# Two-layer transformer blocks on one core: the norms' roots taken on two columns of tokens, and the first blocks of a stage multiplied chunk by chunk

## The chip, the cores and the metric

The kernel runs on one core of one Trainium2 chip. The metric is the device time of one execution in microseconds. The engines named here are TensorE (PE in the profile; its weight loads are the rows PEld), VectorE (DVE), ScalarE (ACT), GpSimd (POOL) and the DMA queue of SyncE (SP).

## The reference, cut to what matters

Two small networks follow one another on 256 tokens of width 1024. Each has two layers, and each layer is: half an ffn, a mixer, half an ffn. Every one of these six parts of a network starts from an RMS norm of the residual stream; the first network also scales and shifts by a modulation vector, and the second ends with one more norm.

```python
def rmsnorm(x, g):
    y = x * lax.rsqrt(jnp.mean(x * x, axis=-1, keepdims=True) + EPS)
    return y * g

def adaln_in(x, g, m, i):
    return rmsnorm(x, g) * (1 + m[:, i, 1][:, None]) + m[:, i, 0][:, None]

def swiglu(h, w1, w3, w2):
    return (jax.nn.silu(h @ w1) * (h @ w3)) @ w2
...
for l in range(DEPTH):
    x = x + 0.5 * m[:, 0, 2] * swiglu(adaln_in(x, norm_g[l, 0], m, 0), ...)
    h = adaln_in(x, norm_g[l, 1], m, 1) @ w_in[l]
    mix = mixer_ab(h, ...) if l % 2 == 0 else mixer_cd(h, ...)
    x = x + m[:, 1, 2] * (mix @ w_out[l])
    x = x + 0.5 * m[:, 2, 2] * swiglu(adaln_in(x, norm_g[l, 2], m, 2), ...)
```

## The kernel before

The work is a list of twelve stages, `STAGES`: ffn, ab, ffn, ffn, cd, ffn for the first network (0 to 5), and ffn, hy, ffn, ffn, sw, ffn for the second (6 to 11). `NSTAGE` (12) is the final norm. The residual `x` lies in SBUF with the 1024 features as 8 chunks of 128 partitions and the 256 tokens in the free direction. The engines run programs of their own, written out by hand and joined by semaphores; there is no scheduler.

**Weights** come as a stream of triples (three blocks of 128 x 1024 f32). SyncE issues a triple into one of two landing places when the one before has been split; ScalarE rounds each block to bf16 (`split_high`, `ring_hi`), VectorE takes the difference (`split_low`, `ring_lo`), and TensorE forms each product as three bf16 products (`product`, lines 392 to 394). The activations are split in the same way into `h_hi` and `h_lo`, `a_hi` and `a_lo`. In stages 0, 2, 3 and 5 VectorE also works off blocks of the modulation weights (`mod_block`).

**A norm of stages 1 to 5 and 12.** As the residual's chunks are updated, ScalarE squares them (`squares`), and TensorE sums the squares over the features with a product of all-ones weights, `sumsq`: eight products of 256 columns into the PSUM bank `pssq`, whose every row then holds the sums of the 256 tokens. VectorE scales them and adds epsilon (line 1192), takes the reciprocal (1193), ScalarE takes the square root (`root`, line 924), and VectorE multiplies `x` by the gain and by `rs` chunk by chunk (line 1330). ScalarE rounds each chunk to `h_hi` (with the shift as its bias), VectorE writes `h_lo` (1335), and TensorE waits for each chunk's `h_ready`. When the stage before is an ffn, two blocks of a ring triple are split ahead of the squares and one behind them. The norm of stage 0 is done by itself at the start. The norms of stages 6 to 11 (`deferred`) multiply by the root only after the product; nothing changes in them.

**An ffn** has 22 steps j. `up(j)` multiplies two weight blocks with h, 24 products of 256 columns for each block, into one of three banks; two steps behind, `down(j)` adds to the eight accumulators. In a deferred ffn step 0 is `up_first`, which takes for each chunk of h the products of both blocks; in stages 0, 2, 3 and 5 step 0 is `up(0)`: the eight chunks for the first block, then the eight for the second.

**Around the two mixers.** Ahead of stage 1 (ab) TensorE makes four products of the bias tables (`filter_start`, line 408), which ScalarE copies out (`bias_rows`, 909); ScalarE also copies out the projected chunks (1071), and a chunk from the third on waits for such a copy. Ahead of stage 4 (cd) TensorE makes a product for the norm of a long filter (431) and its spectrum, eight products of 512 columns (439), before it projects the first chunk; VectorE and ScalarE need both later in the stage.

## Time and profile before

| | |
|---|---|
| median of 3 runs | 2114.94 us (2112.21 to 2116.51) |
| the profiled execution's time | 2119.04 us |
| its span | 2117.3 us |
| TensorE busy | 1912.7 us, 90% |
| VectorE busy | 1436.4 us, 68% |
| ScalarE busy | 989.7 us, 47% |
| DMA | 423.98 MB, mean 200 GB/s |
| mean granted TensorE clock | 0.949 |

### The profile page before, as it was taken

The numbers are of one execution on the slowest core, as the hardware profiler recorded it, in microseconds if no ns is written. First come the engines' busy times: TensorE is split into PE (matmuls) and PEld (weight loads), VectorE is DVE, ScalarE is ACT, GpSimd is POOL, SyncE is SP. The second block draws the span as 40 slices with busy tenths as digits, with TensorE's granted clock in tenths as the row PEclk, the third lists the DMA queues.
The fourth block names the chain that finished last, engine by engine and source line by source line (L and its number), as shares of the span: only waits on it lengthen the run. The fifth ranks groups of instructions, "written<-read, shape, count | busy, mean of one in ns | idle before, by whom it ended". The sixth has DMA issues, their size and how long they took to land.

```text
span 2117.3 us, 38192 instructions
## 1 busy us (share of the span) xinstructions
PE 1912.7 (90%) x16458; PEld 1634.7 (77%) x16458; DVE 1436.4 (68%) x2248; ACT 989.7 (47%) x1591; POOL 6.5 (0%) x14
## 2 busy tenths in 40 slices
PE   3999878999999984799999998779999999969998
PEld 2888667888788862478888887547888888858887
DVE  6889675878798845566576666554766766765664
ACT  3444644445544540344455454324544545464543
POOL 0000000000000000000000000000000000000000
PEclk7999989999999996899999999779999999989999
DMA  8989432776699540336656554203555555432552
GB/s 322 390 339 362 175 149 98 291 281 239 241 366 360 224 182 0 120 143 226 234 181 223 195 193 179 91 30 120 196 195 207 182 207 209 152 118 91 217 200 80
DMA packets 54276, 423.98 MB, mean 200 GB/s; under 512 B 5955, under 2 KB 6131, under 8 KB 26683
## 3 DMA queue, kind: packets, MB, share of 16 engines
q1 hardware_dynamic: 52172, 413.59, 51.9%
q0 software_dynamic: 1936, 7.95, 1.0%
q8 instruction: 130, 2.13, 0.4%
q14 instruction: 38, 0.31, 0.0%
HBM read 420.38 MB, written 1.13 MB: 199 GB/s over the span
## 4 chain that ended last, share of the span: by engine, by line
PE 70%; DVE 16%; ACT 6%; DMA 5%; issue 2%; SPq 0%; DVEq 0%; ACTq 0%
PE pw L392 14%; PE pw L393 14%; PE pw L394 14%; PE acc L392 7%; PE acc L394 7%; PE acc L393 7%; DVE ring_lo L1349 6%; DMA land<-stream 4%; ACT ring_hi L1001 2%; DMA modw<-wmod 1%; PE acc L617 1%; DVE modw L1244 1%; PE pw L582 1%; PE pssq L460 1%; PE pw L585 1%
## 5 line engine op out<-in xcount | busy, mean ns | idle before, releaser
L392 PE MATMUL pw<-h_hi,ring_hi 128*128 128x256 bf16 x3248 | 892.8, 275 | 55.0 <-DVE h_lo L1335 36.5
L393 PE MATMUL pw<-h_lo,ring_hi 128*128 128x256 bf16 x3248 | 892.7, 275 | 0.0
L394 PE MATMUL pw<-h_hi,ring_lo 128*128 128x256 bf16 x3248 | 892.5, 275 | 0.0
L1349 DVE TENSOR_TENSOR ring_lo<-land,ring_hi 128x1024 bf16<-128x1024 f32 x633 | 737.6, 1220 | 191.9 <-ACT ring_hi L1001 191.4
L1001 ACT ACTIVATE ring_hi<-land 128x1024 bf16<-128x1024 f32 x633 | 622.1, 1045 | 234.6 <-DMA land<-stream 120.8
L392 PEld LDWEIGHTS pw<-h_hi,ring_hi 128*128 128x128 bf16 x3248 | 318.5, 98 | 118.8 <-issue 53.1
L392 PE MATMUL acc<-a_hi,ring_hi 128*128 128x256 bf16 x1408 | 384.9, 273 | 4.4 <-DVE a_lo L1399 4.4
L394 PE MATMUL acc<-a_hi,ring_lo 128*128 128x256 bf16 x1408 | 384.8, 273 | 0.0
L393 PE MATMUL acc<-a_lo,ring_hi 128*128 128x256 bf16 x1408 | 384.8, 273 | 0.0
L394 PEld LDWEIGHTS pw<-h_hi,ring_lo 128*128 128x128 bf16 x3248 | 319.7, 98 | 39.8
L393 PEld LDWEIGHTS pw<-h_lo,ring_hi 128*128 128x128 bf16 x3248 | 318.9, 98 | 38.5 <-issue 0.3
L1244 DVE SCALAR_TENSOR_TENSOR modw<-modw,condb 128x1024 f32<-128x1024 f32 x144 | 171.4, 1220 | 13.3 <-DMA modw<-wmod 12.9
L392 PEld LDWEIGHTS acc<-a_hi,ring_hi 128*128 128x128 bf16 x1408 | 137.8, 98 | 21.7 <-DVE a_lo L1399 5.3
L393 PEld LDWEIGHTS acc<-a_lo,ring_hi 128*128 128x128 bf16 x1408 | 137.8, 98 | 16.4
L394 PEld LDWEIGHTS acc<-a_hi,ring_lo 128*128 128x128 bf16 x1408 | 137.8, 98 | 16.5
L1006 ACT ACTIVATE gu<-gu 128x256 f32<-128x256 f32 x88 | 36.7, 417 | 236.3 <-DVE gu L1390 236.3
L1011 ACT ACTIVATE a_hi<-gu 128x256 bf16<-128x256 f32 x176 | 73.3, 416 | 135.1 <-DVE gu L1397 135.1
L1399 DVE TENSOR_TENSOR a_lo<-gu,a_hi 128x256 bf16<-128x256 f32 x176 | 75.0, 426 | 84.8 <-ACT a_hi L1011 84.8
L1009 ACT ACTIVATE gu<-pw 128x256 f32<-128x256 f32 x88 | 33.2, 377 | 127.0 <-PE pw L394 127.0
L1390 DVE TENSOR_TENSOR gu<-pw,rs 128x512 f32<-128x512 f32 x88 | 60.7, 690 | 42.3 <-PE pw L394 42.3
L1397 DVE TENSOR_TENSOR gu<-gu,pw 128x256 f32<-128x256 f32 x88 | 36.7, 417 | 49.8 <-ACT gu L1009 49.5
L1157 ACT ACTIVATE prob<-pw,nbias 128x256 f32<-128x256 f32 (+1 forms) x48 | 20.6, 433 | 105.5 <-DVE nbias L1526 105.5
(230 smaller groups left out, 1557.7 us busy)
## 6 DMA issues: line engine op xcount, KB each, us to landing
land<-stream SPq DMA_DIRECT2D x211, 1536.0 KB, 6.5
modw<-wmod SPq DMA_DIRECT2D x144, 512.0 KB, 7.6
biasT<-bias_rows POOLq DMA_DIRECT2D x3, 1536.0 KB, 9.1
biasT<-bias_rows POOLq DMA_DIRECT2D x1, 3072.0 KB, 13.2
cst_s<-cst SPq DMA_DIRECT2D x1, 1792.0 KB, 10.1
x<-xT SPq DMA_DIRECT2D x1, 1024.0 KB, 9.7
out<-proj SPq DMA_DIRECT2D x1, 1024.0 KB, 3.9
par_s<-par SPq DMA_DIRECT2D x1, 699.0 KB, 13.8
```

The costliest lines, as they stand in the source:

```text
L392: mm(o, lhs[0], rhs[0], start=start, stop=False, skip_group_check=True)
L393: mm(o, lhs[0], rhs[1], start=False, stop=False, skip_group_check=True)
L394: return mm(o, lhs[1], rhs[0], start=False, stop=stop, skip_group_check=True)
L1001: fn(ring_hi[:, t % RING, b, :], land[:, t % LAND, b, :], ACT.Copy).then_inc(hi_ready, 1)
L1006: fn(sig[:, j % 2, :], sig[:, j % 2, :], ACT.Silu).then_inc(silu_done, 1)
L1009: fn(sig[:, j % 2, :], pw[j % (LAG + 1)][:, 0:S], ACT.Silu).then_inc(silu_done, 1)
L1011: fn(a_hi[:, j % (LAG + 1), :], act_in[:, j % 2, :], ACT.Copy).then_inc(a_hi_ready, 1)
L1244: v.scalar_tensor_tensor(modw[:, k % MODR, :], modw[:, k % MODR, :], 1.0, condb[:], ALU.mult, ALU.mult, accum_out=macc[:, g % 2, k:k + 1]) ...
L1349: v.tensor_tensor(ring_lo[:, t % RING, b, :], land[:, t % LAND, b, :], ring_hi[:, t % RING, b, :], ALU.subtract).then_inc(lo_ready, 1)
L1390: v.tensor_tensor(gu[:, j % 2], pw[j % (LAG + 1)][:].rearrange("p (b s) -> p b s", b=2), rs[:].unsqueeze(1).to_broadcast([P, 2, S]), ALU.m ...
L1397: v.tensor_tensor(act_in[:, j % 2, :], sig[:, j % 2, :], up_half, ALU.mult).then_inc(gated_ready, 1)
L1399: v.tensor_tensor(a_lo[:, j % (LAG + 1), :], act_in[:, j % 2, :], a_hi[:, j % (LAG + 1), :], ALU.subtract).then_inc(act_ready, 1)
```

## The change

For the norms of stages 1 to 5 and the final one (`columns(n)`), the squares become the stationary operand and a single column of ones the moving one: the sums come out as two columns, a token to a partition. ScalarE takes the root of scale times sum plus epsilon from PSUM in one instruction, VectorE takes the reciprocal of the 128x2 result, multiplies the identity by each column (`dg`), and TensorE multiplies all-ones weights with these two diagonals (`spread_root`), which puts the inverse root back as rows into `pssq`. The multiplies with the gain read `pssq` instead of `rs`. `spread_root` stands right behind `sumsq` for the ffn stages and the final norm; in stage 1 behind the first of the four table products, in stage 4 between the filter's norm product and its spectrum.

Step 0 of the ffn stages 0, 2, 3 and 5 becomes `up_first`, with a wait for the last ffn's gated halves. In stage 1 the first two projected chunks are made by `first_chunks`, for each chunk of h the products of both.

```diff
             def sumsq(n):
                 for k in range(KD):
                     pe.wait_ge(sq_ready, KD * n + k + 1)
-                    m = mm(pssq[:, 0:S], ones[:], sq[:, k, :], start=(k == 0), stop=(k == KD - 1))
+                    if columns(n):
+                        for tt in range(TT):
+                            m = mm(pssq[:, tt:tt + 1], sq[:, k, tt * P:(tt + 1) * P], ones[:, 0:1],
+                                   start=(k == tt == 0), stop=(k == KD - 1), skip_group_check=True)
+                    else:
+                        m = mm(pssq[:, 0:S], ones[:], sq[:, k, :], start=(k == 0), stop=(k == KD - 1))
                 m.then_inc(ssq_ready, 1)
+            def spread_root(n):
+                pe.wait_ge(diag_ready, column_no(n))
+                for tt in range(TT):
+                    m = mm(pssq[:, tt * P:(tt + 1) * P], ones[:], dg[:, tt, :], start=(tt == 0), stop=True, skip_group_check=True)
+                m.then_inc(bcast_mm, 1)
...
                 mm(pw[2][:], ones[:], f_sq[:, 0, :], start=True, stop=True).then_inc(filt_mm, 1)
+                spread_root(4)
                 spectrum(f_sum, f_dif).then_inc(filt_mm, 1)
...
-                    if j == 0 and deferred(i):
-                        pe.wait_ge(act_ready, f0)
+                    if j == 0:
+                        if f0:
+                            pe.wait_ge(act_ready, f0)
                         up_first()
...
+            def first_chunks(i, kind):
+                t = FIRST[i]
+                for k in range(KD):
+                    pe.wait_ge(h_ready, KD * i + k + 1)
+                    for n in range(2):
+                        if k == 0:
+                            await_triple(t, n + 1)
+                        m = product(bank_of(kind, n)[:, 0:S], weights(t, n, k, slice(0, P)), hidden(k), start=(k == 0), stop=(k == KD - 1))
+                        if k == KD - 1:
+                            m.then_inc(proj_mm, 1)
...
+            def column_root(n):
+                act.wait_ge(ssq_ready, n + 1)
+                fn(rsc[:], pssq[:, 0:TT], ACT.Sqrt, scale=1.0 / D, bias=eps_col[:, 0:1]).then_inc(root_ready, 1)
...
             def root_of(n):
-                dve.wait_ge(ssq_ready, n + 1)
-                rsqrt(("norm", n), rs[:], pssq[:, 0:S], 1.0 / D)
+                dve.wait_ge(root_ready, ROOT["norm", n])
+                done(v.reciprocal(rsc[:], rsc[:]))
+                for tt in range(TT):
+                    ins = v.tensor_scalar(dg[:, tt, :], cs("ident"), rsc[:, tt:tt + 1], None, ALU.mult)
+                ins.then_inc(diag_ready, 1)
+                dve.wait_ge(bcast_mm, column_no(n))
...
-                        v.scalar_tensor_tensor(h[:, k, :], x[:, k, :], g, rs[:], ALU.mult, ALU.mult).then_inc(affine_ready, 1)
+                        v.scalar_tensor_tensor(h[:, k, :], x[:, k, :], g, pssq[:, 0:S] if columns(n) else rs[:],
+                                               ALU.mult, ALU.mult).then_inc(affine_ready, 1)
```

## Rows read from the trace of the kernel before

**Rows 1.** The page's part 1: busy time, share of the span, instructions.
```profile
PE 1912.7 (90%) x16458; PEld 1634.7 (77%) x16458; DVE 1436.4 (68%) x2248; ACT 989.7 (47%) x1591; POOL 6.5 (0%) x14
```

**Rows 2.** Windows, stage 3: stretch, length, busy us of each engine, clock, DMA.
```profile
553.00:720.00 167.00, 167.00 (x1532) 149.45 (x1531) 147.41 (x215) 83.69 (x115) 0.00 (x0) 1.00 0.91 352
```

**Rows 3.** The chain that ended last, in the final norm: start, us, what.
```profile
2107.04 0.43 DVE rs L1192
...
2107.50 1.76 DVE rs L1193
...
2109.29 0.42 ACT rs L924
...
2109.74 0.48 DVE proj L1330
```

**Rows 4.** Timeline of stage 2's start, VectorE and TensorE: start, us, what.
```profile
353.23 0.48 DVE L1335 SCALAR_TENSOR_TENSOR h_lo<-proj,modT,h_hi 128x256 bf16<-128x256 f32 x1
...
357.18 1.27 DVE L1335 SCALAR_TENSOR_TENSOR h_lo<-proj,modT,h_hi 128x256 bf16<-128x256 f32 x3
...
353.85 0.37 PE L392 MATMUL pw<-h_hi,ring_hi 128*128 128x256 bf16 x1 [4.62 <-DVE h_lo L1335]
```

**Rows 5.** Windows over the first 48 products of stages 2, 3, 5; the end of stage 0.
```profile
353.85:362.07 8.22, 8.22 (x48) 4.97 (x49) 4.60 (x12) 4.03 (x8) 0.00 (x0) 0.66 0.62 262
544.68:553.05 8.37, 8.37 (x48) 5.03 (x49) 6.88 (x14) 4.03 (x8) 0.00 (x0) 0.65 0.09 16
917.81:925.65 7.84, 7.84 (x48) 4.76 (x49) 4.60 (x12) 4.02 (x8) 0.00 (x0) 0.69 0.01 2
219.60:222.80 3.20, 3.20 (x17) 2.27 (x16) 1.36 (x4) 2.74 (x6) 0.00 (x0) 0.50 0.93 399
```

**Rows 6.** Timeline, single series of f32 pieces on TensorE, and one of VectorE.
```profile
345.61 3.62 PE L460 MATMUL pssq<-sq,ones 128*128 128x256 f32 x16
...
1842.75 0.60 PE L452 MATMUL pssq<-ones,rs 1*128 1x1 f32 x4
...
320.39 2.05 PE L703 MATMUL acc<-gu,KR 128*128 128x128 f32 x16
...
286.73 3.78 PE L703 MATMUL acc<-gu,prob 128*128 128x128 f32 x16 [4.74 <-DVE gu L1583]
...
299.60 0.87 DVE L1583 TENSOR_SCALAR gu<-cst_s,dn 128x128 f32<-128x128 f32 x4
```

**Rows 7.** Groups of instructions by form: busy us and mean ns of one.
```profile
L1028 ACT ACTIVATE es<-nb,par_s 128x2 f32<-128x2 f32 x24 | 5.6, 279 | 0.0
...
L1537 DVE RECIPROCAL den<-den 128x2 f32<-128x2 f32 x24 | 3.9, 161 | 14.2 <-ACT prob L1157 14.2
...
L1376 DVE SCALAR_TENSOR_TENSOR x<-acc,ada,x 128x256 f32<-128x256 f32 x48 | 20.8, 479 | 24.4 <-PE acc L394 24.4
...
L1330 DVE SCALAR_TENSOR_TENSOR proj<-x,ada,rs 128x256 f32<-128x256 f32 x48 | 22.0, 478 | 2.4 <-ACT rs L924 2.4
```

**Rows 8.** Timeline of stage 1's start, TensorE and ScalarE.
```profile
228.66 3.60 PE L408 MATMUL acc<-biasT,par_s 33*8 33x512 f32 x8
...
241.89 0.62 ACT L1071 ACTIVATE proj<-pw 128x256 f32<-128x256 f32 x2
...
242.39 0.27 PE L392 MATMUL pw<-h_hi,ring_hi 128*128 128x256 bf16 x1 [1.33 <-ACT proj L1071]
```

**Rows 9.** Timeline of stage 4's start, TensorE.
```profile
724.28 1.02 PE L431 MATMUL pw<-proj,ones 128*128 128x512 f32 x2
725.14 3.60 PE L439 MATMUL acc<-qb,cst_s 128*128 128x512 f32 x8
...
732.01 0.27 PE L392 MATMUL pw<-h_hi,ring_hi 128*128 128x256 bf16 x1
```

**Rows 10.** The chain that ended last, in stage 4.
```profile
745.45 0.28 ACT proj L1124
...
745.87 0.22 PE pw L392
```

More of the change, by code:

```diff
@@ L165, in build @@
         den = sb("den", [P, 2, TT])
+        rsc = sb("rsc", [P, TT])
         esink = sb("esink", [P, 2, TT])
@@ L198, in build @@
         f_dif = prob[:].rearrange("p b t s -> p (b t s)").rearrange("p (t c) -> p t c", t=TT)
+        dg = gu[:, 0, 0:1].rearrange("p a (t q) -> p (a t) q", t=TT)
         sig, act_in = gu[:, :, 0, :], gu[:, :, 1, :]
@@ L266, in build @@
         dve_step = sem("dve_step")
+        diag_ready, bcast_mm = sem("diag_ready"), sem("bcast_mm")
         pair_s, pair_b, pair_e, pair_n = sem("pair_s"), sem("pair_b"), sem("pair_e"), sem("pair_n")
@@ L304, in deferred, with columns, column_no @@
             return 6 <= n < NSTAGE
+        def columns(n):
+            return 1 <= n < 6 or n == NSTAGE
+        def column_no(n):
+            return n if n < 6 else 6
         def seen(kind, tt):
@@ L409, in filter_start @@
                        start=True, stop=True).then_inc(filt_mm, 1)
+                    if i == 0:
+                        spread_root(1)
             def filter_layer(l):
@@ L776, in mixer_ab @@
             def mixer_ab(i):
-                for n in range(7):
+                first_chunks(i, "ab")
+                for n in range(2, 7):
                     chunk(i, "ab", n)
@@ L867, in _ @@
                     sumsq(i)
+                    if kind == "ffn":
+                        spread_root(i)
                 if kind == "ffn":
@@ L893, in _ @@
             sumsq(NSTAGE)
+            spread_root(NSTAGE)
         @block.scalar
@@ L921, in root @@
             def root(what, t):
-                act.wait_ge(recip_ready, 6 if what == "filter" else what[1] + 1 + (what[1] > 4))
+                act.wait_ge(recip_ready, 2 if what == "filter" else 1 if what[1] == 0 else what[1] - 3)
                 fn(t, t, ACT.Sqrt).then_inc(root_ready, 1)
+            def column_root(n):
+                act.wait_ge(ssq_ready, n + 1)
+                fn(rsc[:], pssq[:, 0:TT], ACT.Sqrt, scale=1.0 / D, bias=eps_col[:, 0:1]).then_inc(root_ready, 1)
             def inverse_root(dst, src, scale, step):
@@ L981, in norm @@
                         split_high(AFTER[n - 1] - 1 + AHEAD, blocks=(2,))
-                    root(("norm", n), rs[:])
+                    column_root(n)
                 for k in range(KD if n < NSTAGE else 0):
```

## Prediction

> **What bounds the kernel now.** I read the page first: TensorE is busy for 1912.7 of 2117.3 us [rows 1], so time can come only out of its pauses, or out of stretches at its lower clock. Five of the six changed norms stand where it pauses. The windows over the long stretch of the second block's ffn pair show what surrounds a norm: from 553 to 720 us TensorE is busy for 167.00 of 167.00 us at the full clock, although the DMA share is 0.91 [rows 2]. A block that starts sooner therefore ends sooner, as long as weights arrive. I then followed the chain that ended last through one norm, the final one, where nothing overlaps [rows 3]: the squares' products, VectorE's scale-and-add (0.43 us), its reciprocal over 256 elements (1.76), ScalarE's root (0.42), and the first multiply at 2109.74. From 2107.04 to 2109.74 are 2.70 us with TensorE idle. Stages 1 to 5 have the same four steps. Last I read the instructions behind a norm [rows 4]: in stage 2 the first low half is written from 353.23 to 353.71 and the last three by 358.45 (357.18 + 1.27), so the eighth chunk of h is there 4.74 us after the first, and TensorE starts at 353.85. Its first 48 products (both blocks of j = 0) take 8.22, 8.37 and 7.84 us in stages 2, 3 and 5, at a mean clock of 0.66, 0.65 and 0.69 [rows 5], where 48 at the full rate (1532 in 167.00 us is 0.109 each [rows 2]) would need 5.23.
>
> **The change, the chain of one norm.** Out go 2.70 us. In come, one behind another:
> - The sums. Before, 16 pieces (each f32 product is two) took 3.62 us [rows 6]. Now 32 pieces load a 128x128 f32 tile of squares each and move one column. Four pieces with one moving column took 0.60 us, and 16 pieces that load 128x128 and move 128 took 2.05, which gives at most (2.05 - 0.60) / 12 = 0.121 a piece [rows 6]. I take 0.115: 0.60 + 28 x 0.115 = 3.82, that is 0.20 longer. The squares are there in time, as before.
> - The root of two columns on ScalarE: 0.28, like the other 128x2 activation with a bias [rows 7]. In the late stages it is queued behind the third split of a ring block, which is done before the sums are.
> - The reciprocal of 128x2: 0.16 [rows 7].
> - Two 128x128 multiplies of the identity: four such took 0.87 [rows 6], two take about 0.48.
> - The diagonal product, four pieces: between 0.60 (one column each) and 0.60 + 0.10 for the wider ones: 0.70.
> - Handovers: each step starts 0.02 to 0.05 after the one before [rows 3]; five of them, 0.20.
>
> That is 0.20 + 0.28 + 0.16 + 0.48 + 0.70 + 0.20 = 2.02, so a norm's chain is **0.7 us** shorter. Upper bound: a piece at 0.111 and handovers of 0.02 give 0.9. Lower bound: with TensorE at its lower clock 16 pieces took 3.78 instead of 2.05 [rows 6]; four then take 0.5 more, and the gain is 0.2.
>
> The multiplies that use the root now read PSUM. The multiply-add with a PSUM source took 479 ns, the one from SBUF 478 [rows 7], so I cost this at nothing. The Trainium skill (VectorE: DVE Perf Modes, the section on the TRN2 errata) gives PSUM sources 62 cycles more of fixed time; by that each multiply would be some 0.06 us longer, and a norm would lose 0.06 to 0.5 us of its gain. The rows here do not show it.
>
> **The order of the first products.** In ffn stages 2, 3 and 5 all 48 products now follow the arrival of h, six for each chunk. Before, 24 followed it and 24 came behind. The end is now the later of two things: the last chunk plus six products, 4.74 + 0.65 = 5.4 us; or 48 products at the clock granted. Each us at the lower clock costs half a us. Before, 5.6, 5.9 and 4.9 us of these stretches were at half clock (from the means), but much of it was hidden under the waits for h; now it is not. How long will it last? Between 219.6 and 222.8, behind a pause, the products came without gaps at 0.50 [rows 5], and the engine was back at full speed after about that long. I take 3.5 us for dense products: 5.23 + 0.49 x 3.5 = 6.95. The gains are 1.27, 1.42 and 0.89, together **3.6 us**. Bounds: never low, 5.4, gains of 8.2 together; low as long as before, 8.0, 8.1 and 7.6, together 0.7. Stage 0 takes the same order, but ScalarE and VectorE are then splitting triple 1 and DMA bounds the stage: nothing. The second weight block that is now wanted at the first chunk was split one stage earlier, so it adds no wait; and the stricter wait on the a halves refers to the ffn that is over.
>
> **Stage 1 (ab).** TensorE runs the four table products behind the sums, 3.60 us [rows 8]. One stays ahead of the diagonal product, three come after it: they end at about 233.0 instead of 232.3, and the first chunk starts at 233.1, hardly sooner. But chunk 2 waits for ScalarE, whose copies of chunks 0 and 1 start at 241.89 behind the table rows and a triple's split, and TensorE starts again at 242.39 [rows 8]. ScalarE's series begins 0.7 earlier, and the interleaved pair of chunks is done by about 233.1 + 6.95 = 240.1, before it is wanted. Gain 0.7.
>
> **Stage 4 (cd).** Here TensorE does not pause: behind the sums come the norm product at 724.28 and the spectrum from 725.14 to 732.01, then the first chunk at once [rows 9], while h was long begun. The diagonal now stands in the middle of it. It is ready 0.28 + 0.16 + 0.48 + 0.16 = 1.08 after the sums, the norm product covers 0.86 of that, its own pieces take 0.48: with the longer sums the spectrum and the first chunk start 0.20 + 0.22 + 0.48 = 0.9 later, at 732.9. Five chunks of 24 products take 13.1 us and end at 746.0; in the chain the sixth starts at 745.87 [rows 10], released by ScalarE. So VectorE's and the DMA's 0.7 is not used, and I put **-0.1**. If the wait is longer, up to -0.6; if ScalarE's side decides, +0.7.
>
> **Sum.** Stages 1, 2, 3, 5 and the end: 5 x 0.7 = 3.5. First products 3.6. Stage 4 -0.1. Together 7.0 us. The profiled execution took 2119.04 us, 1.7 around its span of 2117.3, and is 4.1 above the median of 2114.94; I take the 7.0 from either: 2112.0 for such an execution, **2108** against the median. In stage 3 weights could become the limit if TensorE gains more than about 2 us on the DMA queue; the share of 0.91 says it is near.
>
> **Rivals.**
> 1. *The clock comes back at once or never falls*, since the pause is shorter and the diagonal product stands in it. 3.5 + 8.2 - 0.1 = 11.6 us, 2103.3. Against it: the pause is still 3.9 us, with 0.5 of work in it.
> 2. *The order brings nothing, or the small steps cost what the large ones did.* With low clock as long as before: 3.5 + 0.7 - 0.1 = 4.1, 2110.8. With 0.2 a norm and 3.6 for the order: 4.5, 2110.4. Both at once: 1.6, 2113.3. This holds most of the outcomes within 0.2%.
> 3. *Slower: weight loads of the squares don't hide.* The sums then cost more in all six norms. The gain of 7.0 over 6 x 28 pieces is gone at 0.115 + 0.042 = 0.157 us a piece, and the time is over 0.2% slower from 0.18. At 0.25, the time of one piece's own pass, it would be 23 us slower, 2138. For it: no row shows 32 one-column pieces that each load 128 rows. Against it: 16 pieces with both a load and 128 columns took 2.05 us, 0.12 each, which leaves no room for load and product one after another. The Trainium skill (TensorE: Matmul & The Clock Gate, the section on the mechanism of row and column tiling) says that a weight load overlaps with products in flight only where the row group differs; here it is the same group, and by that rule each piece would pay load and product. It gives 0.107 us for a load of 128 columns (its section on LDWEIGHTS), so that rule's estimate is some 0.13 to 0.14 a piece for one column, 0.5 to 0.8 a norm, and the gain would fall to 3 us. The trace disagrees with it.
> 4. *Weights bound stage 3*: the order's 1.4 there is lost, 5.6 in all, 2109.3.
>
> **Numbers.** Forecast with rival 4: 0.62. Rival 1: 0.10. Rival 2: 0.22, two fifths of it still over 0.2% (4.2 us, about what a measurement of this kernel tells from no change). Rival 3: 0.05, mostly slower. The range reaches from between the forecast and rival 1 to rival 2's worse case: 2103.5 to 2112.5. Faster 0.77, same 0.19, slower 0.04.
>
> **What would show it.** Right: a chain from the sums' end to the first multiply of 1.8 to 2.1 us instead of 2.70; the 16 pieces replaced by 32 that take 3.7 to 4.0; 48 first products in about 7 us; stage 4's first chunk 0.9 behind its norm's old place. Wrong: sums over 4.5 us; the half clock lasting as long as before under the first products; new waits of TensorE for ring_lo in stage 3; multiplies from PSUM over 0.5 us; or other low stretches in the attention parts, which shift with everything before them.

## The result and the profile after

The change made the kernel slightly slower: 2120.28 us median (14 runs, 2116.01 to 2124.24) against 2116.35 (14 runs) for the kernel before, a ratio of 1.002 with a 95% interval of [1.0011, 1.0029], that is 2.3 to 6.1 us. The forecast was 7.0 us less. One run of an experiment below (wide sums, old order in stage 1) took 5104.41 us where its other eleven took 2107.65 to 2115.43, and is left out everywhere. The profiled execution has a span of 2118.0 us (before 2117.3) at a mean clock of 0.941 (before 0.949). The page's part 1, to be read beside [rows 1]:

```profile
PE 1924.6 (91%) x16578; PEld 1654.2 (78%) x16578; DVE 1426.3 (67%) x2254; ACT 988.0 (47%) x1591; POOL 6.5 (0%) x14
```

VectorE lost 10 us of work, as meant. TensorE is busy for 12 us more. In this execution the sums' 32 pieces take hardly longer than the 16 did (3.63 to 3.80 us against 3.62); the six diagonal products take 7.3 together (six times 1.22); what is left, 4.6, goes with the lower mean clock.

The chain that ended last in the final norm, which answers to [rows 3] (start, us, what):

```profile
2104.73 3.48 PE pssq L476 x32
2108.24 0.27 ACT rsc L972
2108.53 0.18 DVE rsc L1308
2108.73 0.49 DVE gu L1310 x2
2109.27 1.24 PE pssq L486 x4
2110.53 0.48 DVE proj L1382
```

Root, reciprocal and the two multiplies of the identity cost what was forecast (0.27, 0.18, 0.49). The product with the diagonals doesn't: its four pieces take 1.24 us, where 0.70 was put. So from the end of the sums to the first multiply are about 2.3 us. The forecast's terms for that stretch are 1.82 (its 2.02 holds 0.20 for longer sums), and before it was 2.70.

TensorE at the start of stage 1 and of stage 4 (timeline: start, us, engine, line), beside [rows 8] and [rows 9]:

```profile
220.18 3.63 PE L476 MATMUL pssq<-ones,sq 128*128 128x1 f32 x32
223.74 1.46 PE L419 MATMUL acc<-biasT,par_s 33*8 33x512 f32 x2
225.13 1.22 PE L486 MATMUL pssq<-gu,ones 128*128 128x128 f32 x4
226.28 5.29 PE L419 MATMUL acc<-biasT,par_s 33*8 33x512 f32 x6
231.50 0.39 PE L403 MATMUL pw<-h_hi,ring_hi 128*128 128x256 bf16 x1
...
717.96 3.63 PE L476 MATMUL pssq<-ones,sq 128*128 128x1 f32 x32
721.46 1.10 PE L444 MATMUL pw<-proj,ones 128*128 128x512 f32 x2
722.67 1.23 PE L486 MATMUL pssq<-gu,ones 128*128 128x128 f32 x4
723.68 4.73 PE L453 MATMUL acc<-qb,cst_s 128*128 128x512 f32 x8
...
731.68 0.27 PE L403 MATMUL pw<-h_hi,ring_hi 128*128 128x256 bf16 x1
```

ScalarE and TensorE at the third chunk of stage 1, which in [rows 8] starts 16.2 us into the stage (timelines):

```profile
233.95 2.93 ACT L1049 ACTIVATE ring_hi<-land 128x1024 bf16<-128x1024 f32 x3
238.03 0.71 ACT L1119 ACTIVATE proj<-pw 128x256 f32<-128x256 f32 x2 [1.15 <-PE pw L405]
```
```profile
238.56 0.27 PE L403 MATMUL pw<-h_hi,ring_hi 128*128 128x256 bf16 x1 [0.24 <-ACT proj L1119]
```

The sums themselves are as fast here as before (32 pieces in 3.63 us). But what stands behind them is slow: three table products take 5.29 us (all four took 3.60 in [rows 8]), the first half of the spectrum 4.73 instead of 3.60 [rows 9]. The first chunk of stage 4 starts 13.72 us after the sums' start; with the sums in rows it is 11.18 (711.94 to 723.12, in rows shown below for a later kernel whose norm 4 is that of before). Forecast was 0.9 more, it is 2.5 more (2.3 in a second execution). And in stage 1 a new wait has come: ScalarE is through with the table rows and the split, stands idle for 1.15 us until the pair of chunks ends, since both now end together, and only then makes the copy that the third chunk waits for. That one starts 17.3 us into the stage (17.4 in the second execution, where ScalarE's wait is 1.52 us). Before it was 16.2, and 16.5 in a second execution of that kernel.

Windows over the norm of stage 2, the sums, the steps up to the first multiply, the wait for h, and the first 48 products; then the first 48 products of stages 3 and 5 (stretch, length, busy us of PE, PEld, DVE, ACT, POOL, clock, DMA share, GB/s), beside [rows 5]:

```profile
343.75:347.40 3.65, 3.65 (x34) 3.65 (x32) 0.95 (x3) 0.81 (x2) 0.00 (x0) 0.95 0.00 0
347.40:349.91 2.51, 1.37 (x5) 0.99 (x5) 0.65 (x3) 0.26 (x1) 0.00 (x0) 0.50 0.49 80
349.91:351.71 1.80, 0.00 (x1) 0.03 (x1) 1.76 (x5) 1.24 (x3) 0.00 (x0) 0.50 0.90 360
351.71:359.67 7.96, 7.96 (x49) 6.12 (x50) 4.63 (x12) 4.09 (x8) 0.00 (x0) 0.65 0.73 307
541.74:548.57 6.83, 6.83 (x48) 5.43 (x49) 6.83 (x14) 4.08 (x8) 0.00 (x0) 0.76 0.01 2
918.15:926.19 8.04, 8.04 (x49) 6.14 (x50) 4.62 (x12) 4.08 (x8) 0.00 (x0) 0.64 0.00 0
```

The clock falls to 0.50 before the sums have ended (0.95 in the first stretch), so root, diagonal and wait all pass at the lower level. In stage 1 it is much the same: 0.56 between the sums and the end of the diagonal. And the first 48 products take 7.96, 6.83 and 8.04 us where 6.95 was forecast for each.

The same norm in the kernel before, from the start of its sums to the end of the first 48 products in one window:

```profile
345.61:362.07 16.46, 11.84 (x66) 7.86 (x65) 9.55 (x21) 6.55 (x13) 0.00 (x0) 0.79 0.53 199
```

By the mean clocks that is 6.9 us at the lower level before, and over the four stretches above 10.2 after. The norm has become only 0.54 us shorter: about 3.3 us more at half clock cost 1.6 of what the change was meant to give.

In the second execution of the changed kernel (taken for the reason given next) the clock fell earlier still in stage 2, and there the sums themselves are slow. Timeline:

```profile
342.45 4.76 PE L476 MATMUL pssq<-ones,sq 128*128 128x1 f32 x32
```

One profile is not enough to place the loss, so both kernels were profiled in a second execution, unchanged:

> No edit: the kernel before once more. Theory A: stage 0 as long as in the first look, 226.2 us to its last update, stage 1 120.5 and stage 4 188.7. Rival B: stage 0 is 221 to 225 us long as in nearly all other kernels whose stage 0 is the same, stage 1 is 120.5 or 123, stage 4 188.7 to 193.

> No edit: the changed kernel once more, for its stage lengths. Theory A (the length of stages 1 and 4 belongs to the kernel): stage 1 within 0.3 us of 123.6 and stage 4 within 0.5 of 192.3. Rival B (it differs between executions, with the place of the half clock in the attention and the mixer): stage 1 anywhere from 120.9 to 123.6, stage 4 from 189 to 194.

Windows from the last update of the residual in one stage to that of the next, over stages 1 and 4, in the kernel before (two executions), then in the changed one (two):

```profile
226.19:346.69 120.50, 102.43 (x812) 82.89 (x810) 74.59 (x155) 63.79 (x126) 3.17 (x5) 0.92 0.35 132
721.90:910.64 188.74, 133.47 (x855) 100.04 (x854) 104.04 (x178) 60.65 (x112) 1.77 (x2) 0.85 0.25 92
```
```profile
220.66:343.08 122.42, 104.19 (x811) 83.95 (x810) 74.60 (x155) 63.91 (x126) 3.17 (x5) 0.90 0.35 130
717.76:906.33 188.57, 133.16 (x855) 99.99 (x854) 104.06 (x178) 60.64 (x112) 1.77 (x2) 0.85 0.25 92
```
```profile
221.26:344.83 123.57, 107.02 (x832) 85.98 (x832) 72.93 (x155) 63.72 (x126) 3.17 (x5) 0.88 0.35 129
719.04:911.35 192.31, 137.82 (x876) 103.07 (x876) 102.44 (x179) 60.74 (x112) 1.77 (x2) 0.81 0.25 91
```
```profile
221.82:343.53 121.71, 104.62 (x832) 85.18 (x832) 72.96 (x155) 63.57 (x126) 3.17 (x5) 0.92 0.35 131
717.33:909.44 192.11, 137.32 (x876) 102.91 (x876) 102.49 (x178) 60.71 (x112) 1.77 (x2) 0.82 0.24 91
```

Stage 1 differs by 1.9 us between two executions of one program; stage 4 hardly does. Stage 1's difference is 1.2 us in the mean only. Stage 4's 3.6 us are far more than two executions of one kernel differ by here (0.2), but later kernels differ by more: in the kernel with the new order alone, whose stage 4 has no edit, it takes 190.3 us, 1.6 to 1.7 more than in either execution of the kernel before. So the first chunk's 2.3 to 2.5 us are the edit's, and the rest isn't shown to be. Stage 0 takes 226.2 us in the first execution of the kernel before and 220.7 in the second, and over all profiles 218.3 to 225.5 with the new order and 220.7 to 226.2 with the old, so its difference between the two kernels' first profiles (4.9 us) says nothing of the edit. With both executions of each kernel the stages stand so (us, the changed kernel less the one before; from the last updates of x, the end from there to the span's end):

| stage | forecast | measured |
|---|---|---|
| 1 | -0.7 | +1.2 |
| 2 | -2.0 | -0.5 |
| 3 | -2.1 | -0.5 |
| 4 | +0.1 | +3.6 |
| 5 | -1.6 | -0.3 |
| 7 | 0 | +0.5 |
| end | -0.7 | -0.4 |
| sum | -7.0 | +3.6 |

The sum agrees with the medians (+3.9), but partly by luck. Stage 0 is left out of it: with its -1.9 in the mean it would be +1.7. And stage 7, whose norm is a deferred one that the edit doesn't touch, takes 206.3 to 209.1 us over all profiles, so its +0.5 is none of the edit's. Stages 6 and 8 to 11 agree within 0.1.

Stage 3 in the first execution hides something else. Its norm is 1.9 to 2.1 us shorter than before, the stage only 0.2 to 0.4. The chain that ended last near its end, and the timeline of TensorE:

```profile
699.02 8.45 DMA land<-stream
```
```profile
713.37 0.28 PE L403 MATMUL acc<-a_hi,ring_hi 128*128 128x256 bf16 x1 [1.54 <-DVE a_lo L1452]
```

A triple of weights lands at 707.47, ScalarE and VectorE split it, VectorE writes the low half of the gated values only behind that, and TensorE pauses for about 1.7 us from 711.7 on (the row's 1.54 counts from the modelled end of the last product). No such pause stands there in either execution of the kernel before, nor in the second of the changed one, whose norm in stage 3 was 0.6 to 0.8 us shorter. A pause at that place, of 1.7 to 2.3 us, is in five of all 18 profiles, one of them of a kernel whose stage 3 is that of before (186.2 us long instead of 184.1 to 184.3). In three of the five the chain runs through VectorE's modulation blocks and low halves without a landing.

### The profile page after: what moved, and what is told of

The parts are those of the page before. It is cut to its first block, busy times and chain, and to the rows that moved or that the text cites. A ratio compares the mean times of both kernels' runs of the same rounds, so it can differ in the third digit from the quotient of the medians.

```text
span 2118.0 us, 38438 instructions
## 1 busy us (share of the span) xinstructions
PE 1924.6 (91%) x16578; PEld 1654.2 (78%) x16578; DVE 1426.3 (67%) x2254; ACT 988.0 (47%) x1591; POOL 6.5 (0%) x14
## 4 chain that ended last, share of the span: by engine, by line
PE 65%; DVE 18%; DMA 8%; ACT 6%; issue 2%; SPq 0%; DVEq 0%; ACTq 0%
PE pw L403 12%; PE pw L405 12%; PE pw L404 12%; DVE ring_lo L1402 8%; DMA land<-stream 7%; PE acc L403 7%; PE acc L404 6%; PE acc L405 6%; DVE modw L1292 2%; ACT ring_hi L1049 2%; DMA modw<-wmod 1%; PE acc L644 1%; PE pw L609 1%; PE pssq L476 1%; PE acc L453 1%
## 5 line engine op out<-in xcount | busy, mean ns | idle before, releaser
L1402 DVE TENSOR_TENSOR ring_lo<-land,ring_hi 128x1024 bf16<-128x1024 f32 x633 | 737.5, 1219 | 191.6 <-ACT ring_hi L1049 191.1
L404 PEld LDWEIGHTS acc<-a_lo,ring_hi 128*128 128x128 bf16 x1408 | 137.8, 98 | 15.8
```

The costliest lines, as they stand in the source:

```text
L404: mm(o, lhs[0], rhs[1], start=False, stop=False, skip_group_check=True)
L1402: v.tensor_tensor(ring_lo[:, t % RING, b, :], land[:, t % LAND, b, :], ring_hi[:, t % RING, b, :], ALU.subtract).then_inc(lo_ready, 1)
```

## The experiments

All ratios are to the kernel before, run beside on the same chip (medians 2115.6 to 2117.3 us), each from 6 to 12 runs of the experiment; an interval reaches about 0.0009 to 0.0015 to either side. The theory after the result: the one-column sums let TensorE's clock fall ahead of the diagonal, and what stands behind pays for it. The rivals: the order by chunks is what costs; or the diagonal's place in stages 1 and 4, whatever the clock.

### Each part alone

The kernel before with the order by chunks (its norms all in rows):

> The kernel before with the order of the first products alone: step 0 of the four ffn stages and the first two chunks of stage 1 go chunk by chunk, all norms keep their rows. Theory A (the changed kernel loses by its column sums and by where the diagonal product stands, and the order helps): stages 2, 3 and 5 each 0.5 to 1.5 us shorter, stages 1 and 4 unchanged, the time 2 to 4 us under the kernel before, ratio about 0.9985. Rival B (the order itself costs, since all 48 products now run at the clock granted instead of half of them under the waits for h): stages 2, 3 and 5 as long or longer, stage 1 longer, ratio 1.000 to 1.002.

The changed kernel with the old order:

```diff
-                    if j == 0:
+                    if j == 0 and deferred(i):
...
-                first_chunks(i, "ab")
-                for n in range(2, 7):
+                for n in range(7):
```

> The changed kernel with the order of before: column sums, root and diagonal in all six norms, but step 0 and the first chunks block by block. Theory A: stages 1 and 4 lose 3 us and more each, as in the changed kernel's trace (+3.1 and +3.6), and the ffn stages gain at most 0.4 each; ratio 1.003. Rival B: the loss of the changed kernel is gone, ratio 0.998 to 1.000.

Measured: order alone 1.0014 [1.0002, 1.0025], columns alone 1.0014 [1.0006, 1.0023]. Neither part brings anything, and the one forecast at -3.4 us (the columns) costs about 3. By its profile the columns gain 0 to 0.4 us from the sums' start to the first multiply in each norm but that of stage 1, and lose in two places: from the sums' start to the end of the first 48 products stage 1's norm goes from 15.8 to 19.6 us (it was 17.6 in the second execution of the kernel before), stage 4's from 16.4 to 18.7 (16.4 in both). The order alone cost 3 us where it was forecast to gain 3.6, so the expectation's rival B came true by the number. But its profile shows stages 2, 3 and 5 shorter by 0.4, 1.8 and 0.1 us, and stages 1 and 4 longer by 2.7 and 1.6, of which stage 4 isn't changed at all. Why the median doesn't show the gain stays open.

### One column or 128

The changed kernel, where each piece of the sums moves 128 columns of ones into 128 columns of PSUM instead of one; the root reads the first of each:

```diff
-                            m = mm(pssq[:, tt:tt + 1], sq[:, k, tt * P:(tt + 1) * P], ones[:, 0:1],
+                            m = mm(pssq[:, tt * P:tt * P + 128], sq[:, k, tt * P:(tt + 1) * P], ones[:, 0:128],
```

> The changed kernel, but each product of the sums moves 128 columns of ones instead of one, into 128 equal columns of which the root reads one. A piece should take the same 0.11 us, since its weight load sets the distance. Theory C (products of one column do not hold TensorE's clock, so it falls right behind the sums and the diagonal product, the tables and the spectrum run at half clock): the clock falls later, the diagonal's four pieces end in 0.7 us instead of 1.2, stages 1 and 4 get back 2 us and more each; ratio to the kernel before about 0.998 to 1.000. Rival D (the place of the diagonal ahead of tables and spectrum costs that time, whatever the clock; or the clock falls because of the pause): stages 1 and 4 stay about 3 us longer than before, ratio 1.001 to 1.002.

Measured: 0.9982 [0.9968, 0.9996]. 128 times the columns, and 8 us faster than the changed kernel. In its profile stage 1 is 120.3 us long, 2.4 under the changed kernel's mean, and stage 4 191.1, only 1.1 under it where 2 and more were expected. Timeline of its final norm, VectorE, ScalarE and TensorE:

```profile
2098.56 3.74 PE L476 MATMUL pssq<-ones,sq 128*128 128x128 f32 x32
...
2102.83 0.48 DVE L1310 TENSOR_SCALAR gu<-cst_s,rsc 128x128 f32<-128x128 f32 x2
...
2103.37 0.71 PE L486 MATMUL pssq<-gu,ones 128*128 128x128 f32 x4 [1.07 <-DVE gu L1310]
2104.12 1.27 DVE L1382 SCALAR_TENSOR_TENSOR proj<-x,par_s,pssq 128x256 f32<-128x256 f32 x3 [0.80 <-PE pssq L486]
```

The pieces take no longer (3.74 us for 32, the last one's own length counted), the diagonal takes 0.71, and from the sums' start to the first multiply are 5.56 us. The forecast's terms give 3.82 + 0.28 + 0.16 + 0.48 + 0.70 + 0.20 = 5.64: every term of it was right to within 0.1, for a kernel whose clock holds. The changed one needs 5.96 here.

The same with the old order everywhere, and with the old order in stage 1 alone:

> Edit: e3_wide_sums with the old order everywhere (up(0) in stages 0, 2, 3, 5, and block by block in stage 1). Theory A (the order is worth 0.8 + 2 + 2 us in stages 2, 3 and 5, since the half clock under the first 48 products is then shorter): the norms are 16.0, 16.2 and 15.9 us long instead of 15.5, 14.2 and 14.0, and the ratio is 1.000 +- 0.001, some 4 us over e3_wide_sums. Rival B (the order is worth nothing once the clock holds): as e3_wide_sums, 0.998.

> Edit: e3_wide_sums with the first two blocks of stage 1 multiplied one after the other as before. Theory A (the order in stage 1 costs only where it leads to a pause with half clock behind it; in e3_wide_sums it did not): no change against e3_wide_sums, 0.998 +- 0.001, stage 1 within 0.5 us. Rival B (the order in stage 1 is a cost by itself): 2 to 3 us faster than e3_wide_sums, 0.997.

Measured: 0.9986 [0.9975, 0.9996] and 0.9967 [0.9954, 0.998]. The first lost less than was expected (1.000), and the second lies at rival B's number, with theory A's inside its interval. So with the old order, 128 columns instead of one are worth 1.0014 - 0.9986 = 0.0028, some 6 us; the columns as such, with the clock held that far, gain some 3 us on the kernel before, as forecast (3.4).

### The norms of stages 1 and 4

The changed kernel with these two norms in rows, and the same with the old order in stage 1:

```diff
             def columns(n):
-                return 1 <= n < 6 or n == NSTAGE
+                return n in (2, 3, 5, 12)
```

> The changed kernel with the norms of stages 1 and 4 done in rows as before (sums over 256 columns, reciprocal and root over 256 elements, no diagonal); stages 2, 3, 5 and the end keep columns, and the order of the first products stays. Theories A, C and D all say that stages 1 and 4 are back to their old length or a little less, and that the ffn norms still gain 0.2 to 0.6 each: 3 to 5 us under the kernel before, ratio 0.998. If stages 1 and 4 stay long, the cause is the order in stage 1 or something that shifts with time.

> Edit: e4_rows_1_4 with the first two blocks of stage 1 multiplied one after the other as before. Theory A (the order by chunks in stage 1 costs about 3 us behind the norm): stage 1 is 120.5 us long instead of 123.9 in the profile, TensorE's pause for ScalarE 14 us into it is 1.6 instead of 2.5 us, no half clock behind it, and the median is 2 to 3 us under e4_rows_1_4: 0.9985 to 0.999 of before. Rival B (the length of stage 1 is a matter of where the half clock falls in attention, whatever the order): stage 1 is anywhere between 120 and 124, the ratio 1.000 as in e4_rows_1_4.

And the second of them with 128 columns in the sums of the norms that keep columns:

> Edit: the changed kernel with sums that move 128 columns of ones, the norms of stages 1 and 4 in rows as before, and the order by chunks in the four ffn stages alone (stage 1 multiplies block by block as before). Theory A (three separate costs: one-column sums let TensorE's clock fall ahead of the diagonal; the order by chunks in stage 1 ends sooner but is followed by a pause for ScalarE and by a new stretch at half clock, 3 us; in stages 1 and 4 the diagonal stands ahead of other products): all three are gone and what is left are gains in stages 2, 3, 5 and the end, 1.0 + 2.4 + 2.2 + 0.8 = 6.4 us by the norms of e3_wide_sums, so about 2109 against 2115.5, ratio 0.997, and stage 1 as long as before to within 0.3 us. Rival B (what e3_wide_sums gained is where the stretches at half clock happen to fall, not the norms): the median lies anywhere between 2112 and 2118, and the norms' sum does not say where. Rival C (the wide sums alone did it and the rest does not matter): as e3_wide_sums, 0.998.

Measured: 1.0000 [0.9988, 1.0012], 0.9988 [0.9976, 1.0] and 0.9973 [0.9961, 0.9986]. Taking one-column norms out of stages 1 and 4 gives 4 us back; with wide sums (0.9967 against 0.9973) it makes no difference where these two stand. The prediction's cost for the diagonal's place alone, 0.9 us in stage 4, is right when the clock holds: 1.05, see the last experiment.

### The order in stage 1

> Edit: the kernel before with one thing changed: the first two blocks of stage 1 multiplied chunk by chunk. Theory A (by itself a cost: the pair ends sooner, but the third chunk waits for ScalarE's copy as before, so TensorE's pause grows from 1.6 to 2.5 us, and the clock falls behind it): in the profile the pause ends 16.2 us into stage 1 as before, a stretch of 3.4 us at half clock follows at 17, worth 1.7 us, and the median is 2 to 3 us over before, ratio 1.001 to 1.0015. Rival B (chance in where the half clock falls): no difference, 1.000, and no stretch of half clock behind the pause.

The same with filler products in the pause behind the two chunks:

```diff
+            def warm(c):
+                for _ in range(c):
+                    mm(pssq[:, 256:384], ones[:], ones[:], start=False, stop=True, skip_group_check=True)
...
                 first_chunks(i, "ab")
+                warm(10)
```

> Edit: e9_ab_chunks_only with ten f32 products of ones with ones (128 columns, 20 pieces, some 2.3 us, results not used) behind the pair of chunks, in TensorE's pause. Theory A (the cost of the longer pause is the half clock behind it, not the waiting): the stretch at 17 us is gone although TensorE has more to do, and the median is back at that of before, 1.000, 1.5 to 3 us under e9_ab_chunks_only. Rival B (the cost lies elsewhere): as e9_ab_chunks_only or up to 0.5 us more.

Measured: 1.0002 [0.9988, 1.0017] and 1.0006 [0.9992, 1.002]. Theory A isn't borne out: alone, the order in stage 1 costs nothing that these runs can tell from zero (the interval reaches to 3.6 us), its profile shows no half clock behind the pause, and fillers bring nothing. Windows over the pause and what follows, first in the order-only kernel of above, then in the kernel with the order in stage 1 alone, without fillers:

```profile
236.36:238.83 2.47, 0.27 (x4) 0.03 (x2) 2.44 (x4) 2.47 (x5) 1.77 (x4) 1.00 0.60 121
238.83:243.50 4.67, 4.67 (x28) 3.48 (x29) 1.38 (x2) 0.32 (x2) 0.01 (x1) 0.63 0.99 417
```
```profile
234.82:237.07 2.25, 0.27 (x3) 0.03 (x1) 2.21 (x4) 2.25 (x4) 1.54 (x3) 1.00 0.55 122
237.07:241.50 4.43, 4.43 (x41) 3.98 (x42) 1.38 (x2) 0.62 (x3) 0.00 (x0) 1.00 0.99 417
```

Nearly the same pause, and once half clock behind it (28 instructions in 4.67 us), once none (41 in 4.43). The order does make the pause longer (1.6 us before), for ScalarE's copies release the third chunk at the same time whatever TensorE does; whether the clock falls behind it differs between profiles. Two costs of the order have to be kept apart, then: where the clock is low and the pair ends late, both chunks' copies wait for it (the 1.15 us above); where it ends early, as here, nothing but the pause grows. The first of them isn't shown to be the order's at all: in the columns-only kernel, with the old order and the clock as low, the third chunk starts 7.40 us after the first, and in the changed kernel 7.06 and 7.43 us. In pairs the order in stage 1 came out at +0.0002, +0.0012 (the kernel with norms 1 and 4 in rows, less the same with the old order in stage 1) and +0.0015 (the same pair with wide sums and all norms in columns): 0 to 3 us, and its size stays open.

### Holding the clock through the norm

The wide kernel with the old order in stage 1, and filler products in the pauses of stages 2, 3, 5 and the end (results not used):

```diff
+            def warm(c):
+                for _ in range(c):
+                    mm(pw[2][:, 0:128], ones[:], ones[:], start=True, stop=True, skip_group_check=True)
...
                     if kind == "ffn":
+                        warm(4)
                         spread_root(i)
+                        warm(6)
...
             sumsq(NSTAGE)
+            warm(4)
             spread_root(NSTAGE)
```

> Edit: e7_wide_ab_blocks with products of ones with ones (128 columns, to a free bank) in TensorE's pauses of the norms of stages 2, 3 and 5: four between the sums and the diagonal, six behind the diagonal; at the end the four ahead of the diagonal alone. Theory A (what the norms still lose is the half clock under the first 48 products, which falls because TensorE pauses): no half clock under those 48 products, which take 5.5 to 5.9 us instead of 6.6, 8.0 and 8.1, worth some 5 us, ratio 0.9945. Rival B (the pause is too short for it to matter, or the clock falls from what stands in the last products of the stage before): first products as in e7_wide_ab_blocks, 0.997. Rival C (the fillers themselves come late and hold up the diagonal or the first chunk): sums to first multiply over 5.7 us, and slower than e7_wide_ab_blocks.

The same with one moving column in the sums:

> Edit: e11_wide_held with sums that move one column, as in the changed kernel. Theory A (one-column pieces let the clock fall during the sums, before any filler can hold it): the four fillers and the diagonal run at half clock, the fillers themselves then hold the diagonal up, sums to first multiply is 6.5 to 7.5 us instead of 5.6, and in most norms half clock reaches into the first 48 products (6.5 us and more); ratio 0.999 to 1.001, 8 to 12 us over e11_wide_held. Rival B (it was the pause and not the sums that lowered the clock): as e11_wide_held, 0.995.

With all norms in rows, 16 fillers behind the sums of stages 2, 3 and 5:

> Edit: the order by chunks in the four ffn stages, all norms in rows as before, stage 1 as before, and 16 products of ones with ones behind the sums of stages 2, 3 and 5 (3.8 us of a pause of 4.4). Theory A (the clock under the first products is held by any work in the pause, and the column form is then worth only its shorter chain): first 48 products 5.5 to 5.9 us, the norms 15.0 long (before 16.6, 16.6, 16.2), ratio 0.9975, and e11_wide_held is 0.8 us a norm ahead of it, some 3 us in all. Rival B (fillers do nothing): 0.999, the order alone.

With norm 4 in rows:

> Edit: e11_wide_held with the norm of stage 4 in rows as before. Theory A (in stage 4 the first chunk comes 1.05 us later by the diagonal, since TensorE had no pause there): norm 4 is 16.4 instead of 17.5 us long, and the median is 0.5 to 1 us under e11_wide_held, 0.9945. Rival B (ScalarE's side sets stage 4, so that the earlier root is worth more than TensorE's time): 0 to 1 us over it.

Measured, in this order: 0.9950 [0.9937, 0.9964], 0.9994 [0.9981, 1.0007], 0.9981 [0.9967, 0.9994], 0.9950 [0.9935, 0.9965]. With wide sums and the old order everywhere the first 48 products of stages 2, 3 and 5 took 8.58, 7.60 and 8.38 us. The windows show them with wide sums and the new order there, without fillers and with them:

```profile
348.33:354.92 6.59, 6.59 (x49) 5.39 (x50) 4.63 (x12) 4.08 (x8) 0.00 (x0) 0.79 0.94 392
536.58:544.58 8.00, 8.00 (x48) 5.99 (x49) 6.91 (x14) 4.09 (x8) 0.00 (x0) 0.64 0.10 17
911.94:919.99 8.05, 8.05 (x48) 6.16 (x49) 4.63 (x12) 4.08 (x8) 0.00 (x0) 0.64 0.01 2
```
```profile
346.46:352.34 5.88, 5.88 (x49) 4.28 (x50) 4.63 (x12) 4.09 (x8) 0.00 (x0) 1.00 1.01 420
534.01:539.88 5.87, 5.87 (x49) 4.28 (x50) 5.87 (x14) 4.08 (x8) 0.00 (x0) 1.00 0.01 3
905.86:911.73 5.87, 5.87 (x48) 4.29 (x49) 4.63 (x12) 4.09 (x8) 0.00 (x0) 1.00 0.01 3
```

With fillers the clock is 1.00 in all three, and 48 products take 5.87 us. That is the best kernel of the study, 2106.89 us (2104.32 to 2109.9, 6 runs), 10 us under before: ten more products (20 pieces) for each of three norms, four for the last, and faster. What the fillers alone gave is 0.9967 to 0.9950, 3.6 us, and these two intervals overlap; in the profiles stages 2, 3 and 5 are 0.7, 4.0 and 2.2 us shorter, the second of them with the pause at stage 3's end gone (1.8 us). The Trainium skill (TensorE: Matmul & The Clock Gate, the section on how the gate's oscillation bites in real kernels) warns that products in bursts, with waits between them, start each burst at the lower clock. Here the trace agrees (0.64 to 0.79 in the three windows without fillers), and it shows that work without a use in the wait prevents it.

With one-column sums the same fillers bring next to nothing. Windows and timeline over its norm of stage 2:

```profile
338.62:342.30 3.68, 3.68 (x33) 3.68 (x31) 0.95 (x3) 0.81 (x2) 0.00 (x0) 0.90 0.00 0
342.30:345.54 3.24, 3.24 (x16) 3.24 (x16) 0.65 (x3) 0.26 (x1) 0.00 (x0) 0.50 0.54 103
```
```profile
338.62 4.15 PE L476 MATMUL pssq<-ones,sq 128*128 128x1 f32 x32
342.63 2.05 PE L485 MATMUL pw<-ones 128*128 128x128 f32 x8
344.48 1.06 PE L491 MATMUL pssq<-gu,ones 128*128 128x128 f32 x4
345.33 2.77 PE L485 MATMUL pw<-ones 128*128 128x128 f32 x12
```

TensorE is busy without a gap, weight loads as well, and the clock falls all the same while the one-column pieces run (0.90, then 0.50). The sums' last pieces, the fillers (2.05 us where they take 1.06 at the full clock) and the diagonal are late; sums to first multiply is 7.0 us here and 5.8 in stage 3. That settles what lowers it: not the pause alone. Between this kernel and the wide one lie 0.0044, 9 us, for the number of columns that the sums move. What in a one-column piece does it isn't shown.

Rows with fillers (0.9981) are 6.6 us behind columns with fillers, where 3 were expected; a chain that is 0.8 shorter in each of six norms would make 4.8. In the rows kernel's profile stage 3 has the pause of above (2.3 us), which alone could be the rest. Norm 4 in rows or columns makes no difference (0.9950 both), though in rows the first chunk starts 11.18 us after the sums' start and in columns 12.2: 1.05 us that the medians don't tell apart. Timeline of stage 4 with norm 4 in rows, the rows that the comparison above named:

```profile
711.94 3.62 PE L486 MATMUL pssq<-sq,ones 128*128 128x256 f32 x16
...
723.12 0.27 PE L410 MATMUL pw<-h_hi,ring_hi 128*128 128x256 bf16 x1
```

## Why the prediction was wrong

- **The diagonal's cost** was the step that failed, and under it the assumption that TensorE keeps its clock until the diagonal is through. The prediction took 0.70 for its four pieces and kept "with TensorE at its lower clock ... the gain is 0.2" as a bound. They took 1.22 to 1.24 us (1.06 once), so the bound was the rule: from the sums' start to the first multiply the norms gained 0.1 to 0.4 us in the first execution, and in the second those of stages 2 and 5 lost 0.7 and 0.1. The other terms were right: pieces of the sums 0.11 us each (as long as the clock held: 4.76 us for 32 in stage 2 of the second execution), root 0.27, reciprocal 0.18, multiplies 0.49; wide sums gave the forecast chain (5.56 us against 5.64). Of the 10.6 us between forecast and table, 5.4 lie in stages 1 and 4 and 4.4 in stages 2, 3 and 5.
- **What follows the diagonal at that clock** was not in the sum at all. Stage 1's "hardly sooner" first chunk starts 10.2 us into the stage and not 6.9; its pair of chunks ends at 16.9 us and not before it is wanted: ScalarE waits 1.15 us for it, and the third chunk starts 17.3 us into the stage instead of 15.5 (16.2 less the 0.7). Those 1.1 us over the kernel before (1.0 in the mean of two executions each) are about the stage's +1.2, though what follows them in the stage differs by 2 us between executions. Stage 4's 0.9 for the first chunk was 2.5 and 2.3 (1.05 with wide sums), and 3.6 by the stage's end. The part of it behind the first chunk, about 1.2, is half clock that falls elsewhere in the mixer; that the early part causes it was not shown, and it may be no part of the edit's cost, since stage 4 with its norm in rows measured 188.5 to 190.6 us in nine of ten profiles, and 193.9 in the tenth (the first kernel with norms 1 and 4 in rows).
- **The order of the first products**: 3.6 us was over-sized. "3.5 us for dense products" at half clock was read from one stretch; by the mean clocks of the windows it was 5.6, 3.3 and 5.8 us of the first 48 products in stages 2, 3 and 5. Over eight profiles with the new order and no fillers the 48 products took 7.4 us in the mean (6.6 to 8.2; forecast 6.95), over six with the old one 8.2 (7.6 to 8.6): 0.8 a norm, 2.3 us. The medians put it at 4 us with wide sums (0.9986 to 0.9967), with intervals that overlap, and with rows they have the other sign (1.0002 to 1.0014). The lower bound of the time, 5.4, was nearly reached (5.87) where fillers held the clock.
- **Rival 3** (weight loads of the squares don't hide) is refuted in its mechanism: 32 loads of 128 columns and 32 products in 3.63 us, 0.11 a piece. That is under the 0.13 to 0.14 that the prediction estimated by the Trainium skill (TensorE: Matmul & The Clock Gate, the sections on the mechanism of row and column tiling and on LDWEIGHTS). But the sign was its sign: one moving column against the squares as stationary operand cost by the clock, a mechanism that none of the four rivals had. Its price at 0.25 us a piece is also added up wrongly: 168 pieces times 0.135 are 23 us over the forecast's 2108, 2131 and not 2138. And the four chances make 0.99.
- **Rival 2** (the order brings nothing, the small steps cost what the large ones did) came nearest for the norms where TensorE pauses: its worse case was 1.6 us in all, and stages 2, 3, 5 and the end gained 1.7 together. It had nothing for what stages 1 and 4 lost.
- **Rival 1** (the clock never falls) was reached only by adding work. **Rival 4** (weights bound stage 3) held in one of two executions: the pause of 1.7 us behind a landing took back most of that norm's 2. It isn't a fixed limit: with fillers stage 3 is 3.4 us shorter than in the first profile of before in one kernel, and 1.6 in another, which has the pause.
- Multiplies from PSUM cost nothing, as forecast: 474 ns against 478 [rows 7]. The extra cycles of the Trainium skill (VectorE: DVE Perf Modes, the section on the TRN2 errata), weighed in the prediction, don't appear in these times.

## What to carry to other kernels

Moving one column instead of 128 past the same 128x128 weights saved next to nothing here (3.63 us against 3.74 for 32 pieces), and it took TensorE's clock away from everything behind it: look at the granted clock in the windows right behind such a series, not only at its own length. Where a short chain through other engines interrupts TensorE, a few products of constants into a free bank, sized to end before the next real one is due, were worth about as much (0.0017, 3.6 us, on three norms) as the shorter chain on six (some 3 us). With the one-column sums ahead of them they ran at half clock themselves in stage 2, and brought little (0.9994). And the length of a stage is not one number: two executions of one program differed by 1.9 us in one stage and 5.5 in another, as much as the effect looked for. A gain at the start of a stage can also be taken back at its end, as in stage 3, so look for new pauses there too.

## What the hardware showed that was not expected

- Series of 32 pieces with a 128x128 f32 load each: one moving column 3.63 us, 128 moving columns 3.74. In all six norms of both profiles of the changed kernel the clock fell to 0.50 while the first ran or within 1 us behind it; with the second it stayed at 1.00 until the diagonal was through.
- A table product at half clock takes 0.88 us a piece (5.29 us for 6) against 0.45 (2.74 us for 6, in the kernel with wide sums and the old order in stage 1).
- With the same instructions, TensorE's half clock in stages 1 and 4 fell differently from run to run: 120.5 or 123.1 us for stage 1 in two experiments whose stage 1 is the same.
